# Recurrence of a two-block transformer: the last solution's bank products ahead of the second scores, the key norm's steps spread over two weight blocks each, a pair's last outputs behind the next pair's first scores

## The chip, the cores and the metric

The kernel runs on one NeuronCore of one Trainium2 chip. The core has a matrix engine (TensorE, PE in the profile), a vector engine (VectorE, DVE), an activation engine (ScalarE, ACT), a general engine (GpSimd, POOL) and a queue of transfers that SyncE (SP) issues. The metric is the device time of one execution in microseconds.

## The reference

The kernel computes two transformer blocks over 512 tokens of width 1024, all in 32-bit floats. The first block has a recurrence with a delta rule (RWKV7), 12 heads of 64, beside an attention to 256 memory tokens, and then a feed-forward of width 4096. The second has two local attentions with gates and a gated feed-forward. The change touches the recurrence alone, and one number that the plan keeps from there to the end. Cut to what matters:

```python
proj = h @ w_in                                   # 512x1024 by 1024x2560 (and the memory's queries)
slab = proj + (shifted(proj) - proj) * mu         # token shift: each token takes part of the one before
r, k, v, wd, ad, gd = split(slab)                 # r, k, v: 768 each, 12 heads of 64
decay = exp(-exp(-softplus(-(w0 + tanh(wd) @ w2)) - 0.5))
a  = sigmoid(a0 + ad @ a2);  g = sigmoid(gd) @ g2
kk = normalised(k * k_k);    k = k * (1 + (a - 1) * k_a)
for t in range(512):                              # per head, S is 64x64
    S = S * decay[t] + outer(S @ -kk[t], kk[t] * a[t]) + outer(v[t], k[t])
    y[t] = S @ r[t]
y = group_norm(y) * g1 + b1
mix = (y + sum(r * k * r_k) * v) * g
x = x + concat(mix, memory_attention) @ w_out
```

## The kernel before

**Weights.** The weights come in 216 units, most of them 128 rows by 1024 columns. SP loads a unit into `Wraw`, ScalarE casts it to the reduced format fp32r (`Whi`, line 2090), and VectorE or POOL subtracts to get the rest (`Wlo`, line 1643 on VectorE, 2418 on POOL). Cast and subtraction together are one *split*. Its loads run in a ring of `NW` = 3 sets. During the recurrence the plan gives all subtractions to POOL (`state["lo"] = "wlo_pool"`). A unit makes one output tile of 128x512 by eight *weight blocks*; a block is three matmuls of 128x512 (`Hhi,Whi`, `Hlo,Whi`, `Hhi,Wlo`). A tile of kind `slab` is one third (r, k or v, in the plan `projection(p, 0)`, `(p, 1)`, `(p, 2)`) of what a pair of heads needs. When it is done, VectorE scales it (evict, line 1700: `ftmp<-bank,RS`), ScalarE multiplies by a vector (line 2155: `slab<-ftmp,VD`) and VectorE adds the shifted neighbour (`shift`, line 1774: `slab<-ftmp,V,slab`).

**Recurrence.** The 512 tokens are eight chunks of 64 and the 12 heads six pairs (`NP` = 6, `NC` = 8). Inside a chunk the recurrence is solved with products of 64x64, which all lie on line 1047 of PE; one `bank` is a 128x512 piece of PSUM. For a pair the plan has four generators. `inverse(p)` makes the scores (`xm`, `sb`, `na`, `nb`, `vn`, `kn`, `sk`), a triangular inverse in six levels (`t1`, `xt`, `xu` with the level's number), `gv`, and at its end `yu`, a level product. `states(p)` makes the last solution `uw` (`GA,Yi`), the increments `pd`, the transfers `phi`, the outputs in chunks `yo1`, seven state steps `st`, in each of which PE waits for the state `PD` of the step before (line 1915), and the outputs from the states, `yo2`. `tail(p)` makes the group norm (`gsq`, `root t`, `tn`), the gate `tg` (`GD,g2s`) and the result `tlo`. `bonus(p)` is the step `bo`. `ahead(p + 1)` prepares the next pair: the three projections, and between them `sg` and `ta` (decay and rate), the square of the key (`sq`), the running sum of the decays (`cum`, the scan of line 1791), `exps`, `kf`, the root of the key norm (`root f`), `kk` and `ops` (four VectorE instructions of the operands, lines 1805 to 1820, and the product kf*Pi on POOL, line 2476). VectorE masks what PE has written: line 1829 (`BR<-bank,C`) reads the second scores `sb`, line 1879 makes `T`, line 1886 makes `Xi`, both for a level of the inverse.

**Order.** The plan is one list of steps, made at build time; each engine runs its part of the list in order, and waits on semaphores where a step needs another engine's result. `two("sb", p)` takes two of the five PSUM banks of ring `M`, in turn, so a step waits also for the bank's former user to be read out. `inverse(p)` sets the pace: each `yield` of it gives a number of microseconds, and `blend` lets the filler emit as many steps as fit in that number times `FILL_PAIR`. The filler alternates (`turns`) between two lines of steps: bonus, states and tail of the pair behind, and `ahead(p + 1)`. In the loop over pairs, what is left of the filler is emitted at the end of the pair:

```python
gens = [itertools.chain(bonus(p), *((states(p - 1), tail(p - 1)) if p else ())), ahead(p + 1)]
filler = turns(*gens)
blend(inverse(p), filler, FILL_PAIR[p])
run(filler)
```

A split is put in the list when a unit begins: `splits(u + state["ahead"])`. With `ahead` = 2 (`NW - 1`) the split of the next unit is queued then, with 3 (`NW`) that of the one behind it. The five stretches of the loop are called pairs here: the first lies at 64 to 107 us, the others at about 107, 156, 204 and 253 us to 303 us.

Of the kernel before, what the change touches and what calls it, by code (L numbers as in the profile page):

```python
# [14 lines left out]
NP = 6  # L15
# [3 lines left out]
FILL_PAIR = (1.05, 1.35, 1.35, 1.35, 1.35)  # L19
# [6 lines left out]
NW = 3  # L26
# [34 lines left out]
class Plan:  # L61
# [9 lines left out]
    def step(self, kind, *key):  # L71
        self.steps.append((kind, *key))
        self.count(kind, *key)
# [55 lines left out]
def run(gen):  # L129
    for _ in gen:  # L130
        pass


def turns(*gens):
    gens = list(gens)
    while gens:
        for g in list(gens):
            try:
                yield next(g)
            except StopIteration:  # L140
                gens.remove(g)
# [31 lines left out]
def blend(main, filler, per):  # L173

    due = 0.0
    for room in main:
        due += per * room
        while due > 0:
            took = next(filler, None)
            if took is None:  # L180
                break
            due -= took


def couples(tile):

    for _ in tile:
        next(tile, None)
        yield 1.6
# [7 lines left out]
def make_plan(units):  # L197
# [9 lines left out]
    state = {"loads": 0, "splits": 0, "units": 0, "lo": "wlo", "ahead": 1, "held": None}  # L207
# [29 lines left out]
    def bank(kind, *key):  # L237

        M.take((kind, *key))
        step(kind, *key)  # L240
        M.give((kind, *key))
# [94 lines left out]
    def shift(t):  # L336

        step("shift", t)
        ftmp.give(("shift", t))
# [118 lines left out]
        yield from pipeline([item(n) for n in range(8)])  # L458

    def projection(p, i):  # L460
        state["held"] = held = []
        yield from couples(tile("slab", (p, i), ("rw", 6 * i + p), "x", range(8)))
        state["held"] = None
        yield 0
        shift(held[0])

    def rates(p):

# [14 lines left out]
    def bonus(p):  # L483
        step("bo", p)
        ftmp.give(("sq", p))
        yield 1.0

    def ahead(p):

        k = projection(p, 1)  # L490
        for _ in range(4):
            yield next(k)
        yield from rates(p)
        yield from k
        square(p)
        r = projection(p, 0)
        yield next(r)
        decays(p)
        yield next(r)
        step("exps", p)  # L500
        step("kf", p)
        bank("root", "f", p)
        yield 0.9
        yield from r
        v = projection(p, 2)
        yield next(v)
        bank("kk", p)
        yield 0.5
        yield next(v)
        step("ops", p)  # L510
        yield next(v)
        yield from v

    def inverse(p):

        two("xm", p)
        yield 1.4
        two("sb", p)
        yield 0.9
        two("na", p)  # L520
        yield 0.7
        for kind in ("nb", "vn", "kn"):
            bank(kind, p)
            yield 0.7
        two("sk", p)
        step("ai", p)
        yield 1.0
        for l in range(1, len(LEVELS)):
            if l == 3:
                two("gv", p)  # L530
                yield 0.7
            two("t1", p, l)
            if l > 1:
                two("xt", p, l - 1)
            yield 1.6
            if l < len(LEVELS) - 1:
                two("xu", p, l)
                yield 1.4
        bank("yu", p)
        yield 1.2  # L540

    def states(p, room=0.2):

        two("uw", p)
        yield 1.0
        two("pd", p)
        yield 0.5
        two("phi", p)
        yield 0.6
        two("yo1", p)  # L550
        yield 0.6
        for ch in range(1, NC - 1):
            step("st", p, ch)
            yield room
        bank("yo2", p)
        yield 0.9

    def tail(p):
        step("gsq", p)
        yield 0  # L560
        bank("root", "t", p)
        yield 0.9
        yield 0
        bank("tn", p)
        yield 0.5
        yield 0
        bank("tg", p)
        yield 1.0
        step("tlo", p)
        count("Ulo", "mix", p)  # L570
        yield 0


    def values_and_queries():
        yield from projection(0, 2)
        for i in range(2):
            yield from couples(tile("qm", (i,), ("rw", 20 + i), "x", range(8)))

# [26 lines left out]
    filler = between()  # L605
# [7 lines left out]
    state["lo"] = "wlo_pool"  # L613
    mem_att = mem_attention()
    mix_order = (0, 1, 2, 3, 4, 6, 7, 5)
    for p in range(NP - 1):
        gens = [itertools.chain(bonus(p), *((states(p - 1), tail(p - 1)) if p else ())), ahead(p + 1)]
        filler = turns(*gens)
        blend(inverse(p), filler, FILL_PAIR[p])
        run(filler)  # L620

    outs = [tile("res", ("gffn", i), ("wo", i), "mix", mix_order, js=mix_order, own=i == 2) for i in range(3)]

    def beside():
        yield from turns(itertools.chain(bonus(NP - 1), states(NP - 2), tail(NP - 2)), mem_att)
        step("Xload")
        for i, g in enumerate(outs):

            state["ahead"] = (NW - 1, NW, NW - 1)[i]
            yield from spaced(itertools.islice(g, 7), 0.8)  # L630
        state["ahead"] = NW - 1

    filler = beside()
    blend(itertools.chain(inverse(NP - 1), states(NP - 1, 0.6), spaced(tail(NP - 1), 1)), filler, FILL_LAST)
# [82 lines left out]
    filler = some_gates(range(8))  # L717
# [14 lines left out]
    filler = side_b()  # L732
# [2017 lines left out]
```

## Time and profile before

| | us |
|---|---|
| median of three runs | 1522.12 |
| lowest, highest | 1521.64, 1524.64 |
| the profiled execution | 1518.95 |
| its span in the trace | 1517.2 |

| engine | busy us | share of the span | instructions |
|---|---|---|---|
| PE, matmuls | 1462.2 | 96% | 11374 |
| PEld, weight loads (beside PE) | 1156.8 | 76% | 11374 |
| DVE | 800.4 | 53% | 1261 |
| ACT | 552.7 | 36% | 942 |
| POOL | 239.4 | 16% | 166 |

The span is the time from the first to the last record of the core; the profiled execution's own time is 1.75 us above it. The share of an engine is the mean over all stages. A wait of PE is idle time that the profile puts down to what came last, as in `[1.79 <-DVE BR L1829]`. The granted clock (PEclk) is 1.00 at 2.4 GHz and 0.50 at 1.2 GHz; over the whole span it is 0.997.

### The profile page before, as it was taken

Reading aid. Unit: us, or ns where it says so; the run is one execution under the profiler, and the core shown is the slowest. Engines: PE = TensorE matmul, PEld = TensorE weight load, DVE = VectorE, ACT = ScalarE, POOL = GpSimd, SP = SyncE. Lnnn points to the kernel's source line nnn. Section 1 sums busy time; section 2 is a strip of 40 time slices with the busy share of each in tenths; the row PEclk is TensorE's granted clock in tenths of the full one; section 3 lists DMA queues with packets and bytes.
Section 4 is the critical chain, followed back from the end, with each engine's and each line's share of the span. In section 5 each row is a group of like instructions: output and inputs, shape, how many; then the busy total and the mean of one; then the engine's idle time right before and its main releaser. Section 6 shows DMA issues by size and latency. Waiting matters only on the chain.

```text
span 1517.2 us, 26650 instructions
## 1 busy us (share of the span) xinstructions
PE 1462.2 (96%) x11374; PEld 1156.8 (76%) x11374; DVE 800.4 (53%) x1261; ACT 552.7 (36%) x942; POOL 239.4 (16%) x166
## 2 busy tenths in 40 slices
PE   7999999979999999999999999999999999999999
PEld 6867777756788888888788766767777888888887
DVE  5655566664564444535644358577554443443343
ACT  7444434363422221312442256545333221222221
POOL 0233333201200000000110012222322210220120
PEclk9999999999999999999999999999999999999999
DMA  8311011011223232333233133311222333323223
GB/s 323 112 30 44 30 30 44 23 52 58 70 87 108 84 108 87 98 97 97 84 97 96 58 107 96 94 56 53 83 92 89 97 97 98 97 85 109 84 88 107
DMA packets 39334, 130.89 MB, mean 86 GB/s; under 512 B 4272, under 2 KB 5296, under 8 KB 39216
## 3 DMA queue, kind: packets, MB, share of 16 engines
q1 hardware_dynamic: 39216, 129.18, 26.9%
q8 instruction: 90, 1.47, 0.4%
q14 instruction: 28, 0.23, 0.0%
HBM read 127.07 MB, written 2.10 MB: 85 GB/s over the span
## 4 chain that ended last, share of the span: by engine, by line
PE 82%; DVE 8%; ACT 4%; issue 3%; POOL 0%; POOLq 0%; ACTq 0%; DVEq 0%
PE bank L1047 79%; PE bank L1447 1%; DVE Wlo L1643 1%; ACT Whi L2090 1%; DVE qa L1754 1%; DVE z L1680 0%; DVE Xi L1886 0%; DVE qa L1752 0%; ACT Hhi L2171 0%; PE bank L1161 0%; DVE X L1725 0%; ACT kbr L2337 0%; ACT slab L2306 0%; PE bank L1237 0%; ACT tmpb L2205 0%
## 5 line engine op out<-in xcount | busy, mean ns | idle before, releaser
L1047 PE MATMUL bank<-Hhi,Whi 128*128 128x512 f32 x912 | 375.8, 412 | 11.6 <-DVE Wlo L1643 8.4
L1047 PE MATMUL bank<-Hhi,Wlo 128*128 128x512 f32 x912 | 360.9, 396 | 0.0
L1047 PE MATMUL bank<-Hlo,Whi 128*128 128x512 f32 x912 | 357.6, 392 | 0.0
L1047 PE MATMUL bank<-Uhi,Whi 128*128 128x512 f32 x736 | 290.9, 395 | 8.1 <-POOL Wlo L2418 3.1
L1047 PE MATMUL bank<-Uhi,Wlo 128*128 128x512 f32 x736 | 287.2, 390 | 0.0
L1047 PE MATMUL bank<-Ulo,Whi 128*128 128x512 f32 x736 | 287.0, 390 | 0.0
L2090 ACT CAST Whi<-Wraw 128x1024 fp32r<-128x1024 f32 (+1 forms) x216 | 222.9, 1036 | 164.2 <-PE bank L1047 148.2
L1643 DVE TENSOR_TENSOR Wlo<-Wraw,Whi 128x1024 fp32r<-128x1024 f32 (+1 forms) x175 | 224.2, 1282 | 98.9 <-ACT Whi L2090 98.8
L1047 PEld LDWEIGHTS bank<-Hhi,Whi 128*128 128x128 f32 x912 | 171.5, 188 | 66.0 <-issue 12.3
L1047 PEld LDWEIGHTS bank<-Hlo,Whi 128*128 128x128 f32 x912 | 171.9, 188 | 42.1
L1047 PEld LDWEIGHTS bank<-Hhi,Wlo 128*128 128x128 f32 x912 | 172.0, 189 | 34.0 <-issue 1.2
L1047 PEld LDWEIGHTS bank<-Uhi,Whi 128*128 128x128 f32 x736 | 138.1, 188 | 45.2 <-DVE Wlo L1643 5.5
L1047 PEld LDWEIGHTS bank<-Ulo,Whi 128*128 128x128 f32 x736 | 138.3, 188 | 29.4
L1047 PEld LDWEIGHTS bank<-Uhi,Wlo 128*128 128x128 f32 x736 | 138.3, 188 | 27.8 <-issue 0.2
L2418 POOL TENSOR_TENSOR Wlo<-Wraw,Whi 128x1024 fp32r<-128x1024 f32 x41 | 99.8, 2433 | 367.1 <-ACT Whi L2090 366.4
L1725 DVE TENSOR_TENSOR X<-X,bank 128x512 f32<-128x512 f32 x72 | 49.5, 688 | 168.8 <-PE bank L1047 168.7
L2426 POOL TENSOR_TENSOR accb<-accb,tmpb 128x512 f32<-128x512 f32 x14 | 18.8, 1344 | 383.9 <-ACT tmpb L2205 383.9
L2165 ACT CAST Uhi<-tmpb 128x512 fp32r<-128x512 f32 x32 | 19.8, 619 | 148.0 <-DVE tmpb L1734 148.0
L2431 POOL TENSOR_TENSOR qa<-qa 128x512 f32<-128x512 f32 x22 | 28.5, 1295 | 198.9 <-ACT qa L2175 198.9
L2179 ACT CAST Hhi<-qa 128x512 fp32r<-128x512 f32 x22 | 13.7, 622 | 116.0 <-POOL qa L2436 116.0
L2347 ACT ACTIVATE sr<-sr,st 128x256 f32<-128x256 f32 (+1 forms) x64 | 33.7, 528 | 36.6 <-DVE st L2015 19.8
L1732 DVE SCALAR_TENSOR_TENSOR tmpb<-bank,RSb 128x512 f32<-128x512 f32 x32 | 22.1, 692 | 44.8 <-PE bank L1047 44.6
(292 smaller groups left out, 1571.8 us busy)
## 6 DMA issues: line engine op xcount, KB each, us to landing
Wraw<-in_wts SPq DMA_DIRECT2D x208, 512.0 KB, 3.5
bA<-in_biasA SPq DMA_DIRECT2D x12, 256.0 KB, 2.8
Wraw<-in_wts SPq DMA_DIRECT2D x8, 384.0 KB, 3.2
x<-in_xT SPq DMA_DIRECT2D x8, 256.0 KB, 4.4
x_rows<-in_xN SPq DMA_DIRECT2D x2, 1024.0 KB, 8.3
X<-in_xT SPq DMA_DIRECT2D x2, 1024.0 KB, 7.2
out<-X SPq DMA_DIRECT2D x8, 256.0 KB, 2.1
bB<-in_biasB SPq DMA_DIRECT2D x4, 384.0 KB, 3.1
```

The source lines that it names most:

```text
L1047: return e.matmul(o, lhsT, rhs, start=start, stop=stop, skip_group_check=True)
L1447: p = e.transpose(o, sr[n % 3][:, x:x + 128], c("ident"))
L1643: e.tensor_tensor(Wsp[k][1][:, 0:width], Wraw[k][:, 0:width], Wsp[k][0][:, 0:width].bitcast(F), ALU.subtract).then_inc(S["wlo"])
L1725: e.tensor_tensor(y, y, z, ALU.add).then_inc(S["evict"])
L1732: e.scalar_tensor_tensor(z[:], b[:], 0.0, RSb[:], ALU.max, ALU.mult).then_inc(S["evict"])
L1754: e.tensor_tensor(z[:], z[:], gates[i], ALU.add).then_inc(S["gated"])
L2090: e.copy(Wsp[k][0][:, 0:width], Wraw[k][:, 0:width]).then_inc(S["whi"])
L2165: e.copy(Uhi[:, x.key[1], :], tmp_of(("raw", t))[:]).then_inc(S["ffhi"])
L2347: p = e.activation(part, part, ACT.Exp, scale=1.0, bias=x[:, 2 + i:3 + i], accum_out=x[:, 4 + i:5 + i])
L2418: done(e.tensor_tensor(Wsp[k][1][:, 0:width], Wraw[k][:, 0:width], Wsp[k][0][:, 0:width].bitcast(F), ALU.subtract), "wlo_pool")
L2426: done(e.tensor_tensor(accb[:], accb[:], tmp_of(("sqr", *x.key))[:], ALU.add), "sq_add")
L2431: done(e.tensor_tensor(z[:], z[:], s[:], ALU.mult), "sig")
```

## The change

It has five parts.

1. `inverse(p)`: for all pairs but the last, the room behind `xm` goes from 1.4 to 2.0 and that behind `sb` from 0.9 to 0.3. The filler's step `uw` of the pair behind then stands between the two weight blocks and `sb`, in place of behind `sb`.
2. `ahead(p)`: k, r and v are generators whose steps are couples of two weight blocks, and every other step of the next pair stands behind one couple. `read_out` finishes a tile and emits its evict; the shift comes behind the next tile's first couple.
3. The loop over pairs emits at a pair's end only what is left of the projections. What is left of the chain (bonus, states, tail) goes on beside the next pair's first steps. The last state steps, `yo2`, `gsq` and `root t` then have other neighbours among the weight blocks.
4. `values_and_queries`, ahead of the first pair, gets the same form.
5. `state["ahead"]` is `NW` from the end of the recurrence on, in place of `NW - 1`.

```diff
--- before.py
+++ after.py
@@ -458,11 +458,14 @@
         yield from pipeline([item(n) for n in range(8)])
 
     def projection(p, i):
+        return couples(tile("slab", (p, i), ("rw", 6 * i + p), "x", range(8)))
+
+    def read_out(projected):
+
         state["held"] = held = []
-        yield from couples(tile("slab", (p, i), ("rw", 6 * i + p), "x", range(8)))
+        run(projected)
         state["held"] = None
-        yield 0
-        shift(held[0])
+        return held[0]
 
     def rates(p):
 
@@ -487,36 +490,40 @@
 
     def ahead(p):
 
-        k = projection(p, 1)
+        k, r, v = (projection(p, i) for i in (1, 0, 2))
         for _ in range(4):
             yield next(k)
         yield from rates(p)
-        yield from k
+        t = read_out(k)
+        yield next(r)
+        shift(t)
         square(p)
-        r = projection(p, 0)
-        yield next(r)
         decays(p)
         yield next(r)
         step("exps", p)
         step("kf", p)
+        yield next(r)
         bank("root", "f", p)
-        yield 0.9
-        yield from r
-        v = projection(p, 2)
+        yield next(r)
+        t = read_out(r)
+        yield next(v)
+        shift(t)
         yield next(v)
         bank("kk", p)
-        yield 0.5
         yield next(v)
         step("ops", p)
         yield next(v)
-        yield from v
+        t = read_out(v)
+        yield 0
+        shift(t)
 
     def inverse(p):
 
         two("xm", p)
-        yield 1.4
+
+        yield 2.0 if p < NP - 1 else 1.4
         two("sb", p)
-        yield 0.9
+        yield 0.3 if p < NP - 1 else 0.9
         two("na", p)
         yield 0.7
         for kind in ("nb", "vn", "kn"):
@@ -572,7 +579,11 @@
 
 
     def values_and_queries():
-        yield from projection(0, 2)
+        v = projection(0, 2)
+        yield from itertools.islice(v, 4)
+        t = read_out(v)
+        yield 0
+        shift(t)
         for i in range(2):
             yield from couples(tile("qm", (i,), ("rw", 20 + i), "x", range(8)))
 
@@ -613,22 +624,25 @@
     state["lo"] = "wlo_pool"
     mem_att = mem_attention()
     mix_order = (0, 1, 2, 3, 4, 6, 7, 5)
+    rest = iter(())
     for p in range(NP - 1):
-        gens = [itertools.chain(bonus(p), *((states(p - 1), tail(p - 1)) if p else ())), ahead(p + 1)]
-        filler = turns(*gens)
-        blend(inverse(p), filler, FILL_PAIR[p])
-        run(filler)
+
+        chain = itertools.chain(rest, bonus(p), *((states(p - 1), tail(p - 1)) if p else ()))
+        projections = ahead(p + 1)
+        blend(inverse(p), turns(chain, projections), FILL_PAIR[p])
+        run(projections)
+        rest = chain
 
     outs = [tile("res", ("gffn", i), ("wo", i), "mix", mix_order, js=mix_order, own=i == 2) for i in range(3)]
 
     def beside():
-        yield from turns(itertools.chain(bonus(NP - 1), states(NP - 2), tail(NP - 2)), mem_att)
+        yield from turns(itertools.chain(rest, bonus(NP - 1), states(NP - 2), tail(NP - 2)), mem_att)
         step("Xload")
         for i, g in enumerate(outs):
 
             state["ahead"] = (NW - 1, NW, NW - 1)[i]
             yield from spaced(itertools.islice(g, 7), 0.8)
-        state["ahead"] = NW - 1
+        state["ahead"] = NW
 
     filler = beside()
     blend(itertools.chain(inverse(NP - 1), states(NP - 1, 0.6), spaced(tail(NP - 1), 1)), filler, FILL_LAST)
```

On PE, at the start of a steady pair: `ftmp,C` is the bonus `bo`, the `Hhi`/`Hlo` rows are the first of two weight blocks (the second reads the same), `AR,ta` is `sb`, `GA,Yi` is `uw`, `C,AR` is `na`. Before:

```order
L1047 MATMUL bank<-GD,g2s 128x512
L1047 MATMUL bank<-ta,AR_125 64x64 x16
L1047 MATMUL bank<-ftmp_76,C 128x512
L1047 MATMUL bank<-Hhi,Whi_61 128x512
L1047 MATMUL bank<-Hhi,Wlo_62 128x512
L1047 MATMUL bank<-Hlo,Whi_61 128x512
...
L1047 MATMUL bank<-AR_125,ta 64x128 x16
L1047 MATMUL bank<-GA_108,Yi_109 64x128 x16
L1047 MATMUL bank<-C,AR_125 64x64 x16
```

After:

```order
L1061 MATMUL bank<-ta,AR_125 64x64 x16
L1061 MATMUL bank<-ftmp_76,C 128x512
L1061 MATMUL bank<-Hhi,Whi_61 128x512
L1061 MATMUL bank<-Hhi,Wlo_62 128x512
L1061 MATMUL bank<-Hlo,Whi_61 128x512
...
L1061 MATMUL bank<-GA_108,Yi_109 64x128 x16
L1061 MATMUL bank<-AR_125,ta 64x128 x16
L1061 MATMUL bank<-C,AR_125 64x64 x16
```

`uw` now stands ahead of `sb`; the gate product `GD,g2s` stood ahead of `xm` (`ta,AR`) before, and stands ahead of `yu` (`Yi,T`) now.

On PE, at the end of the pair before that: the last rows are a weight block, `yu` (`Yi,T`), `tg` (`GD,g2s`), `xm` and `bo`. Before:

```order
L1047 MATMUL bank<-Hhi,Whi_59 128x512
L1047 MATMUL bank<-Hhi,Wlo_60 128x512
L1047 MATMUL bank<-Hlo,Whi_59 128x512
L1047 MATMUL bank<-Yi_109,T_119 64x64 x16
L1047 MATMUL bank<-GD,g2s 128x512
L1047 MATMUL bank<-ta,AR_125 64x64 x16
L1047 MATMUL bank<-ftmp_76,C 128x512
```

After (`Xi,MT` is the last `t1`, `C,Xi` the last `xt`, the first `C,z` is the sum of `root t` and the second, on another line, the mean `tn`):

```order
L1061 MATMUL bank<-Xi,MT 64x64 x16
L1061 MATMUL bank<-C,Xi 64x64 x16
L1061 MATMUL bank<-C,z_106 128x128 x4
L1175 MATMUL bank<-C,z_106 128x128 x4
L1061 MATMUL bank<-GD,g2s 128x512
L1061 MATMUL bank<-Yi_109,T_119 64x64 x16
L1061 MATMUL bank<-ta,AR_125 64x64 x16
```

The weight block that stood right ahead of `yu` is gone from there; between the last `t1` and `xm` PE has bank products only.

On DVE, around the scan of the next pair's decays (`sg<-C,sg`), with the state steps `PD`, the evict `ftmp<-bank,RS` and the shift. Before:

```order
L1915 SCALAR_TENSOR_TENSOR PD<-bank,PC_89,PD 128x64
L1700 TENSOR_TENSOR ftmp_77<-bank,RS 128x512
L1915 SCALAR_TENSOR_TENSOR PD<-bank,PC_89,PD 128x64
L1774 SCALAR_TENSOR_TENSOR slab_69<-ftmp_77,V,slab_69 128x511
L1879 TENSOR_TENSOR T_119<-bank,C 128x4x64 x2
L1915 SCALAR_TENSOR_TENSOR PD<-bank,PC_89,PD 128x64
L1791 SCALAR_TENSOR_TENSOR sg<-C,sg 128x512
L1886 TENSOR_TENSOR Xi<-bank,Xi 128x4x64 x2
```

After:

```order
L1929 SCALAR_TENSOR_TENSOR PD<-bank,PC_89,PD 128x64
L1714 TENSOR_TENSOR ftmp_77<-bank,RS 128x512
L1893 TENSOR_TENSOR T_119<-bank,C 128x4x64 x2
L1929 SCALAR_TENSOR_TENSOR PD<-bank,PC_89,PD 128x64
L1788 SCALAR_TENSOR_TENSOR slab_69<-ftmp_77,V,slab_69 128x511
L1805 SCALAR_TENSOR_TENSOR sg<-C,sg 128x512
L1900 TENSOR_TENSOR Xi<-bank,Xi 128x4x64 x2
L1929 SCALAR_TENSOR_TENSOR PD<-bank,PC_89,PD 128x64 x2
```

Before, the mask `T` and a state step stood between the shift and the scan; now the shift and the scan stand next to each other, behind the mask and one state step more.

On ScalarE, at the same place, the square of the key (`ftmp<-slab`) stood between the multiply `slab<-ftmp` and the cast `Whi` of the next unit. Now the cast comes right behind the multiply, and the square behind it and a copy of `Yi`.

## Rows read from the trace of the kernel before

**Rows 1.** Stretches of three pairs: length, busy us per engine, PEclk, DMA, GB/s.

```profile
64.00:107.09 43.09, 41.07 (x756) 32.17 (x758) 24.47 (x51) 17.95 (x35) 13.20 (x11) 1.00 0.17 52
...
204.20:252.81 48.61, 45.08 (x965) 34.98 (x964) 30.40 (x65) 20.26 (x40) 16.11 (x12) 1.00 0.11 35
252.81:302.97 50.16, 46.63 (x966) 36.27 (x965) 30.40 (x65) 20.26 (x40) 16.10 (x12) 0.97 0.09 25
```

**Rows 2.** Waits of PE, 107 to 303 us: total us, times, longest.

```profile
PE bank L1047 <- DVE BR L1829: 7.2, 4, 1.8
PE bank L1047 <- DVE PD L1915: 3.8, 4, 1.0
PE bank L1047 <- DVE Xi L1886: 2.7, 4, 0.7
```

**Rows 3.** Timeline from 204 us: start, length, engine, operation, [idle before].

```profile
207.27 1.10 PE L1047 MATMUL bank<-AR,ta 64*64 64x128 f32 x32
...
210.46 0.76 DVE L1829 TENSOR_TENSOR BR<-bank,C 128x256 f32<-128x256 f32 x2
...
211.03 0.69 PE L1047 MATMUL bank<-C,AR 64*64 64x64 f32 x32 [1.79 <-DVE BR L1829]
```

**Rows 4.** Timeline, 224 to 227 us, the first state steps of a pair.

```profile
224.34 0.29 PE L1047 MATMUL bank<-PD,AR 64*64 64x64 f32 x4
...
225.26 0.27 DVE L1915 SCALAR_TENSOR_TENSOR PD<-bank,PC,PD 128x64 f32<-128x64 f32 x1
...
225.59 0.33 PE L1047 MATMUL bank<-PD,AR 64*64 64x64 f32 x4 [0.96 <-DVE PD L1915]
...
226.16 0.72 ACT L2155 ACTIVATE slab<-ftmp,VD 128x512 f32<-128x512 f32 x1
```

**Rows 5.** Timeline, 242 to 252.6 us, the end of that pair.

```profile
242.56 2.38 POOL L2418 TENSOR_TENSOR Wlo<-Wraw,Whi 128x1024 fp32r<-128x1024 f32 x1 [8.32 <-ACT Whi L2090]
...
243.15 0.69 PE L1047 MATMUL bank<-T,Yi 64*64 64x64 f32 x32
...
243.55 1.67 DVE L1680 COPY z<-st 128x512 f32<-128x512 f32 x1
...
245.28 0.66 PE L1161 MATMUL bank<-C,z 128*128 128x128 f32 x4
...
246.60 0.69 PE L1047 MATMUL bank<-Xi,MT 64*64 64x64 f32 x32 [0.67 <-DVE Xi L1886]
...
247.69 0.50 PE L1047 MATMUL bank<-Hhi,Whi 128*128 128x512 f32 x1
...
247.91 0.75 DVE L1879 TENSOR_TENSOR T<-bank,C 128x256 f32<-128x256 f32 x2
...
248.57 0.68 DVE L1820 TENSOR_TENSOR AR<-kn,Pp 128x512 f32<-128x512 f32 x1
...
250.38 0.74 DVE L1805 SCALAR_TENSOR_TENSOR ftmp<-slab,V,kf 128x512 f32<-128x512 f32 x1
...
251.25 1.27 POOL L2476 TENSOR_TENSOR kf<-kf,Pi 128x512 f32<-128x512 f32 x1 [4.02 <-DVE ftmp L1805]
```

**Rows 6.** Timeline, 101 to 104 us and 229 to 233 us.

```profile
101.64 1.29 POOL L2470 TENSOR_TENSOR ta<-ta,kn 128x512 f32<-128x512 f32 x1
...
101.92 1.55 DVE L1820 TENSOR_TENSOR AR<-kn,Pp 128x512 f32<-128x512 f32 x1
...
229.06 1.21 DVE L1791 TENSOR_TENSOR_SCAN sg<-C,sg 128x512 f32<-128x512 f32 x1
...
229.51 2.92 POOL L2418 TENSOR_TENSOR Wlo<-Wraw,Whi 128x1024 fp32r<-128x1024 f32 x1 [2.39 <-ACT Whi L2090]
```

**Rows 7.** Waits of PE, 372 to 1517 us.

```profile
PE bank L1047 <- POOL Wlo L2418: 6.2, 4, 1.7
PE bank L1047 <- DVE Wlo L1643: 2.8, 3, 1.8
```

**Rows 8.** The stretch with the low granted clock, columns as in rows 1.

```profile
262.00:264.00 2.00, 2.00 (x9) 1.70 (x9) 0.00 (x0) 0.26 (x1) 0.00 (x0) 0.50 0.49 195
```

## The prediction, made before the changed kernel ran

> **What bounds the kernel now.** I read the totals of five stretches first. TensorE (PE) is busy in about 93% of a pair [rows 1], so the end can only move by the stretches in which PE stands. The first pair of heads lies at 64 to 107 us; of the next four, three take 48.6 us and the last 50.16. The list of waits for those four pairs has three entries that repeat in all four [rows 2]: 7.2 us for the BR mask, 3.8 us for the state PD, 2.7 us for Xi. I call them gaps A, B and C. In order of time they are 1.79 us before the `na` products [rows 3], 0.96 us before the second state product [rows 4], 0.67 us before the last `t1` [rows 5]. Together 1.79 + 0.96 + 0.67 = 3.42 us a pair. Behind 372 us, PE's waits for a split weight are 6.2 + 2.8 us [rows 7].
>
> **Part 1, solution ahead of second scores.** `uw` now takes the two banks behind `tn` and `tg`, `sb` takes one behind `yu` and one behind `xm`, and `na` waits for the second `xm` bank and the first `uw` bank. All these are read out early, so `na` no longer waits for VectorE's (DVE's) seven `sb` masks. What is late next: `vn` takes the first `sb` bank and needs six of the seven masks. Before, the masks end at 210.46 + 0.76 = 211.22, about 2.8 us behind the end of `sb` (207.27 + 1.10) [rows 3]; the sixth ends some 0.35 us sooner. Between `sb` and `vn` PE now has `na` (0.69), two weight blocks (about 1.5) and `nb` (about 0.4), so at most 0.1 us of gap A stays. `uw` also needs the sum Yi behind `yu`; DVE does it some 5.0 us behind the start of `tn`, and PE comes to `uw` at 5.8. Gain 1.7 us a pair; bounds 0.9 (Yi a DVE step late) to 1.79.
>
> **Part 2, one chain step later.** The second state product moves from right behind the first to behind two weight blocks, `t1` and `xt`, about 2.6 us, against the 1.2 us that it needs from first product to PD [rows 4]. Gap B goes: 0.96 us, bounds 0.8 to 0.96.
>
> **Part 3, the end of a pair.** Before, four weight blocks stand between the last `xt` and `yu`; now two of them stand ahead of the last `t1`, and the other two further forward. So behind the last block PE has `t1`, `xt`, `root t`, `tn`, `tg`, `yu`, `xm` and nothing to fill. Call S the start of the last `xu`. PE: from S to behind two blocks 245.28 - 243.15 = 2.13 us, `t1` and `xt` 247.69 - 246.60 = 1.09, `root t` about 1.2: idle from S + 4.4 [rows 5]. DVE: Xi from about S + 0.75 to S + 1.45, then the four of `ops`, from 248.57 to 250.38 + 0.74 = 2.55 us, which now stand ahead of the last mask: S + 4.0; mask 0.75: S + 4.75; then reciprocal and the copy into z, which without a disturbance takes 0.4 us (one measured 1.67 only since a split of POOL stood beside it) [rows 5]. POOL's kf*Pi starts 0.13 behind `ops` and takes 1.27 [rows 5], so it is over at S + 5.4, and the copy ends at about S + 5.75. `tn` starts at S + 5.8: a new wait of 1.4 us where gap C was 0.67. I take 1.5, bounds 0.9 (the mask hides some) and 2.7 (copy as before, 1.67). Gap C goes, since between `xu` and `t1` no key multiply stands ahead of Xi any more. In the first pair the end costs about the same as the 1.04 and 0.70 us that PE waits there now (not shown apart: 43.09 - 41.07 = 2.0 us idle [rows 1]).
>
> **Part 4, POOL's split beside the scan.** This is the step that decides. Shift and square of the key come later, but the cast of the next weight stays right behind the key's first slab. In ScalarE's queue the square no longer stands ahead of the cast. The slab starts at 226.16 [rows 4], the cast follows about 0.65 later and POOL's subtraction (Wlo) 1.1 after that: 227.9, not 229.51 as now [rows 6]. DVE then has, back to back, PD, the shift (slab<-ftmp,V,slab) from about 227.8 and the scan. Both read two tensors of SBUF. What such an overlap does: AR<-kn,Pp took 1.55 us beside a POOL multiply that had started 0.28 earlier [rows 6], and 0.68 alone [rows 5]; it ended 0.54 behind POOL. The other way round, Wlo beside the scan took 2.92 us, where another took 2.38 [rows 6, 5]. So whoever is first holds the other up. If the shift is first, by 0.1 us, Wlo stands waiting while it runs, and I expect it to be next: Wlo from about 228.5 to 230.9 and the scan over at about 232.0, where alone it would end at 229.7. Xi and the next PD stand behind it on DVE: PD at 233.0, and the fourth state product, whose slot on PE is at 231.9, waits 1.2 us. If Wlo is first the shift waits and the wait is 1.0. If DVE keeps its hold over both, none. I take 1.2 us, bounds 0 and 2.4 (a whole Wlo). In the first pair there is no state product, but the exponents and with them the key norm's copy and a mask come 2.3 us later: about 0.9 us more.
>
> The Trainium skill, "SBUF — State Buffer", section "Who interferes with whom", says that a DVE instruction with two SBUF inputs contends with a GpSimd one that reads SBUF, and elsewhere on that page that the first to start holds the shared ports for the whole instruction. The 1.55 us of [rows 6] agree. By that rule the change loses its 1.2 us; without it, none.
>
> **Part 5, casts one weight earlier.** From here on each split is queued a whole weight ahead of its use. What PE can gain is its two shorter waits for DVE's Wlo, 2.8 - 1.8 = 1.0 us [rows 7], some four of 0.1 at 740 to 780, and of the waits for POOL's Wlo near 1100 (the longest is 1.7 us) little: there POOL holds up DVE's gate sums, and PE would next wait for DVE's evictions, so I take 0.4. The 1.8 us wait at 392 stays: two splits in place of one stand behind the same three evictions. Sum 1.8 us; bounds 0 and 6.
>
> **Sum.** The profiled execution took 1518.95 us (span 1517.2). Four pairs: 4 x (3.42 - 0.1 - 1.5 - 1.2) = 2.5 us; first pair -0.9; part 5 +1.8. Saved 3.4, so 1515.5 for an execution like that one. The median of the timed runs is 3.17 us above it: 1518.7. The clock fell once in the pairs, to 0.50 (1.2 GHz) at 262 to 264 us [rows 8], behind a gap A, and that pair took 50.16 instead of 48.61 [rows 1]. With gap A gone I give that 1.55 us half a chance to go: 0.8. **Forecast 1518.0 us.** The term with the widest bounds is the fourth. With parts 1 to 3 at the better ends, part 4 at 0 and part 5 at 1.8, 4 x 2.5 + 1.8 + 0.8 = 12.6 us are saved: 1509.5. With part 4 at 2.4 and part 3 at 2.7, 4 x (3.42 - 0.1 - 2.7 - 2.4) - 0.9 + 1.8 = -6.2: 1528.3.
>
> **Rivals.** (a) *DVE keeps its hold, the scan isn't delayed.* For it: the shift starts, by my times, just ahead of Wlo, and the scan follows it with no wait. Against: when DVE's hold ends, POOL has been waiting. Then 4 x (3.42 - 0.1 - 1.5) + 1.8 + 0.8 = 9.9: 1512.2 us.
> (b) *The end of a pair is worse than 1.5 us.* z's copy stands beside a POOL instruction as long as now, 1.67 instead of 0.4, in four pairs: 5 us against (a) or the forecast. Against: no split is due there, since the cast behind the last slab comes later. With part 4 at its forecast the four pairs gain nothing, -0.9 + 1.8 + 0.8 = 1.7 less 2.5: 1522.9; with part 4 at 0 it is 1517.3.
> (c) *Slower: the clock.* From the last `t1` to `bo` PE now has some 7 us with a wait in it and no weight block. A gap of 1.8 us was followed by half clock in one pair of four [rows 1, 8], priced 1.55 us. Should the clock fall twice in each of the five pairs, 10 x 1.55 = 15.5 less the forecast's 3.4: 1534. It decides from three falls on: 3.4 us saved and 2 x 1.55 more than now. Against: the wait is shorter than gap A, and B is gone.
> (d) *It doesn't do what it says.* The order shows the moved products; banks alone could still hold `uw` back if `tn`'s read-out on DVE is late (part 1's margin is 0.8 us). Then A is only moved: 4 x 0.9 less than forecast, 1521.6.
>
> **How the numbers follow.** Forecast as summed: 0.47; (a) 0.28; (b) 0.09; (c) 0.08; (d) 0.08. 0.2% of 1522 is 3.0 us, about what a measurement of this kernel tells from no change. The forecast stands 4.1 us below, and its own range of 1515 to 1521 lies two thirds under that bound; with (a) that gives faster 0.63, same 0.26 (a third of the forecast, most of (b) and (d)), slower 0.11. The range takes in (a) and most of (b) and (d) and leaves out (c): 1511 to 1523.
>
> **What would show it.** Right: no PE wait behind the BR mask, nor for PD behind the first state product; a PE wait of 1.3 to 1.6 us for the copy into z at each of four pair ends; the scan or the shift at 2 us or more instead of 1.2 or 0.75, with Wlo across it, and a PE wait for PD of about 1.2 us; pairs of about 47.8 us. Pairs of 46.6 us with a 2.9 us or longer Wlo mean (a). Pairs of 48.6 us or more, with a granted clock under 1, mean (c). Wrong in any case: a wait at `uw`, or pair spans over 49 us at full clock.

## The result: 1508.37 us, faster by 0.96%, outside the forecast range

| | median us | lowest, highest | runs |
|---|---|---|---|
| before | 1523.03 | 1521.64, 1524.64 | 4 |
| after | 1508.37 | 1507.47, 1509.41 | 4 |

The ratio is 0.9904, with a 95% interval of 0.9886 to 0.9921. A second set of runs of the same kernel gave 1509.69 against 1522.02, 0.9919 (0.9905 to 0.9934). The gain is 12 to 15 us; the forecast had 4, and a lowest value of 1511. The profiled execution of after took 1509.15 us (span 1507.3), 9.8 us less than that of before.

The totals of the stretches in after (columns as in [rows 1]): the first pair with 5 us of what lies ahead of it, a steady pair, and the last pair up to the second output tile.

```profile
64.00:107.82 43.82, 41.53 (x755) 32.61 (x754) 26.14 (x52) 19.26 (x37) 13.57 (x11) 1.00 0.20 60
201.45:248.26 46.81, 44.66 (x971) 34.66 (x969) 30.97 (x66) 20.50 (x40) 16.54 (x12) 1.00 0.12 37
...
295.04:386.18 91.14, 77.12 (x1360) 56.75 (x1356) 50.42 (x122) 40.91 (x95) 12.94 (x8) 0.96 0.10 32
```

A pair takes 46.8 us where [rows 1] has 48.61. PE waits 1.3 us less in it, and its own busy time is 0.42 us less (45.08 to 44.66). PE's waits from 107 to 295 us in after answer to [rows 2]:

```profile
PE bank L1175 <- DVE z L1694: 5.4, 4, 1.4
PE bank L1061 <- DVE PD L1929: 3.1, 4, 0.8
PE bank L1061 <- DVE T L1893: 1.4, 1, 1.4
```

The waits behind BR, for the first PD and for Xi are gone. In their place stand two: 1.35 us for z's copy at each pair's end, and 0.78 us for a later PD. (The single wait for T is the end of the first pair.) The timeline of after at the start of a pair answers to [rows 3]:

```profile
204.57 1.10 PE L1061 MATMUL bank<-GA,Yi 64*64 64x128 f32 x32
...
205.50 1.05 PE L1061 MATMUL bank<-AR,ta 64*64 64x128 f32 x32
...
206.47 0.69 PE L1061 MATMUL bank<-C,AR 64*64 64x64 f32 x32
...
208.64 0.76 DVE L1843 TENSOR_TENSOR BR<-bank,C 128x256 f32<-128x256 f32 x2
...
210.27 0.35 PE L1061 MATMUL bank<-GA,BR 64*64 64x64 f32 x8
```

`uw`, `sb` and `na` follow each other with no wait, and the last two masks of `sb` (208.64) are done before anything needs them. The next place is around the scan, in the same view; it answers to [rows 4, 6]:

```profile
223.46 0.74 DVE L1788 SCALAR_TENSOR_TENSOR slab<-ftmp,V,slab 128x511 f32<-128x511 f32 x1
223.59 2.85 POOL L2432 TENSOR_TENSOR Wlo<-Wraw,Whi 128x1024 fp32r<-128x1024 f32 x1 [0.78 <-ACT Whi L2104]
...
224.12 3.42 DVE L1805 TENSOR_TENSOR_SCAN sg<-C,sg 128x512 f32<-128x512 f32 x1
...
228.10 0.27 DVE L1929 SCALAR_TENSOR_TENSOR PD<-bank,PC,PD 128x64 f32<-128x64 f32 x1
...
228.42 0.33 PE L1061 MATMUL bank<-PD,AR 64*64 64x64 f32 x4 [0.78 <-DVE PD L1929]
```

The shift starts 0.13 us ahead of POOL's subtraction and takes 0.74 us (0.75 where nothing stands beside it, in e11 below). The scan behind it takes 3.42 us in place of 1.21: it ends 1.1 us behind the subtraction, as if it had begun only when that was over. And at the end of a pair, answering to [rows 5]:

```profile
244.06 0.75 DVE L1893 TENSOR_TENSOR T<-bank,C 128x256 f32<-128x256 f32 x2
244.28 1.26 POOL L2490 TENSOR_TENSOR kf<-kf,Pi 128x512 f32<-128x512 f32 x1 [3.29 <-DVE ftmp L1819]
...
245.02 0.20 DVE L1691 RECIPROCAL st<-st 128x8 f32<-128x8 f32 x1 [0.20 <-ACT st L2147]
245.25 0.57 DVE L1694 COPY z<-st 128x512 f32<-128x512 f32 x1
...
245.97 0.63 PE L1175 MATMUL bank<-C,z 128*128 128x128 f32 x4 [1.35 <-DVE z L1694]
```

PE's waits behind 366 us in after. Those for POOL's `Wlo` of [rows 7] (6.2 us) are not in the list; others, for VectorE's gate sums, stand at the same places, so that these lists alone show no gain (13 us in both kernels). The wait for `sr`, 2.2 us here, is 0.4 us in before (last row).

```profile
PE bank L1061 <- DVE qa L1766: 2.9, 2, 1.6
...
PE bank L1061 <- DVE sr L2016: 2.2, 1, 2.2
PE bank L1061 <- DVE Wlo L1657: 1.8, 1, 1.8
PE bank L1061 <- DVE Hlo L1770: 1.8, 1, 1.8
```

```profile
PE bank L1047 <- DVE sr L2002: 0.4, 1, 0.4
```

### The profile page after: what moved, and what is told of

Same layout as the page of the kernel before. It is cut to its first block, busy times and chain, and to the rows that moved or that the text cites. A ratio compares the mean times of both kernels' runs of the same rounds, so it can differ in the third digit from the quotient of the medians.

```text
span 1507.3 us, 26652 instructions
## 1 busy us (share of the span) xinstructions
PE 1458.5 (97%) x11374; PEld 1157.6 (77%) x11374; DVE 809.5 (54%) x1261; ACT 554.1 (37%) x942; POOL 241.5 (16%) x166
## 3 DMA queue, kind: packets, MB, share of 16 engines
q8 instruction: 90, 1.47, 0.4%
## 4 chain that ended last, share of the span: by engine, by line
PE 85%; DVE 7%; ACT 2%; issue 2%; POOL 0%; POOLq 0%; ACTq 0%; DVEq 0%
PE bank L1061 82%; PE bank L1461 1%; DVE sg L1805 1%; DVE qa L1768 1%; PE bank L1175 1%; DVE qa L1766 0%; ACT Hhi L2185 0%; DVE Wlo L1657 0%; PE bank L1418 0%; ACT kbr L2351 0%; ACT slab L2320 0%; PE bank L1251 0%; DVE T L1893 0%; ACT Whi L2104 0%; DVE Xi L1900 0%
```

## The experiments

All ratios are to before, from runs on the same chip, made together. A *fall* is a stretch in which the granted clock is 0.50 (1.2 GHz). The theory after the result was: the order of `uw` carries nearly all of the pairs' gain, falls of the clock that follow gap A carry the rest, and parts 2 to 4 cancel. Its rivals: that before's profiled execution was merely a quick one, and that the new order of the whole pair is what helps.

### c0: the kernel before, again

No edit.

> The unchanged kernel, to see how its executions differ. The profiled execution of before took 1518.95 us and its timed runs 1521.6 to 1524.6, while after has 1507.5 to 1509.4 with its profiled one among them. Theory (clock): each wait of 1.8 us behind the second scores is followed by a fall to half clock in some executions; the profiled one had 1 in four pairs, the others have 2 to 4 in the pairs, at 1.55 us each. Then a run of 1523 shows a mean granted clock about 0.001 lower per 1.6 us, 0.994 to 0.996 where the first showed 0.997. Rival (other): the clock is 0.997 in slow and quick runs alike and the 4 us lie in waits.

Measured: 1521.13 us (1518.65 to 1523.75, 12 runs) against 1521.55, 0.9998 (0.9988 to 1.0009). Of the 32 executions of before in this set, those with a mean granted clock of 0.995 or less (14 of them) took 1522.9 us on average, those with 0.997 or more (14 too) 1519.3, and four lie between. So the kernel before has two groups of executions, and the profiled one of the forecast (0.997, 1518.95) was of the quick one. The profiled execution here has its fall at another place, behind the third gap A, and its pair takes 50.13 us where its neighbours take 48.55:

```profile
204.59:254.72 50.13, 46.60 (x965) 36.28 (x964) 30.41 (x65) 20.26 (x40) 16.08 (x12) 0.97 0.11 34
212.00:214.00 2.00, 2.00 (x13) 1.57 (x6) 0.00 (x0) 0.65 (x2) 1.32 (x2) 0.61 0.40 94
214.00:216.00 2.00, 2.00 (x10) 1.74 (x9) 0.00 (x0) 0.43 (x1) 0.00 (x0) 0.54 0.45 176
```

The theory's price holds (1.55 to 1.6 us a fall); that the longer executions have their falls in the pairs is not shown, since only profiled executions show where a fall lies.

### e1 and e2: part 5 alone

```diff
 # e1, from after
-        state["ahead"] = NW
+        state["ahead"] = NW - 1
```

```diff
 # e2, from before
-        state["ahead"] = NW - 1
+        state["ahead"] = NW
```

> After, with only the casts' distance behind the recurrence put back (2 in place of 3). In the traces the two kernels lie 5.87 us apart from 392 to 740 us and 9.8 us at the end. Theory (casts): those 3.9 us are part 5's, so this kernel is 3 to 4.5 us slower than after, 1511.3 to 1512.9, and the waits for Wlo of POOL near 1100 (6.2 us in all) are back. Forecast's own figure: 1.8 us, 1510.2. Rival (chance of one execution): under 1 us apart, since the clock fell elsewhere there.

> Before, with only the casts' distance behind the recurrence changed (3 in place of 2). Theory: as large as in e1 with the sign turned, 3 to 4.5 us under before, 1518.5 to 1520. Rival (forecast): 1.8 us. Rival (chance): under 1 us.

Measured: e1 1512.43 us (1510.68 to 1514.03), 0.9937 (0.9922 to 0.9952), which by the ratios is 2.7 us above the second set of after and 5.0 above the first; e2 1518.23 us (1516.28 to 1519.86), 0.9977 (0.9966 to 0.9988), 3.3 us under before. Part 5 is worth 3.3 us or a little more, not 1.8: of the executions with a mean granted clock of 0.995, three of e1 take 1513.7 us on average and three of after 1509.6. Where it lies is seen in the same work in both traces (the first two rows are of before, the last two of after; the first of each starts at the same weight block, and so does the second):

```profile
724.32:982.40 258.08, 254.16 (x1281) 194.43 (x1280) 144.70 (x226) 118.38 (x219) 33.32 (x17) 1.00 0.30 91
1160.51:1517.20 356.69, 352.83 (x1537) 287.87 (x1535) 142.57 (x154) 88.74 (x108) 56.53 (x44) 1.00 0.30 95
```

```profile
718.45:974.71 256.26, 252.33 (x1281) 195.38 (x1280) 143.96 (x225) 118.12 (x219) 33.24 (x17) 1.00 0.30 91
1152.50:1507.30 354.80, 351.59 (x1537) 288.31 (x1535) 143.23 (x153) 87.95 (x107) 56.33 (x44) 1.00 0.30 94
```

1.82 and 1.89 us less, and this is no chance of two executions. From the first matmul of each stretch to the first behind it, or to the last of all, the four traces without part 5 take 258.1 us (c0, with a fall, 259.6) and 352.8 to 353.1; the ten traces with it take 256.2 to 256.3 and 351.3. In both stretches it is mostly PE's *busy* time that shrinks (1.83 and 1.24 us), though the matmuls are the same. A split that comes a little late doesn't stand in the list of waits; it stretches the distance of two matmuls. Before:

```profile
739.33 1.63 DVE L1643 TENSOR_TENSOR Wlo<-Wraw,Whi 128x1024 fp32r<-128x1024 f32 x1 [0.60 <-ACT Whi L2090]
...
740.50 0.39 PE L1047 MATMUL bank<-Ulo,Whi 128*128 128x512 f32 x1
...
741.02 0.50 PE L1047 MATMUL bank<-Uhi,Whi 128*128 128x512 f32 x1
...
741.36 0.39 PE L1047 MATMUL bank<-Uhi,Wlo 128*128 128x512 f32 x1
```

The subtraction ends at 740.96, and the two matmuls behind it start 0.52 and 0.34 us after the matmul ahead of each, in place of 0.23. No wait of PE is listed there. At the same two places e1 has 0.52 and 0.34 too, e2 and after 0.23 and 0.23. The beginnings of the seven weights between 735 and 770 us make 1.5 of the first stretch's 1.82 us in this way. In the second stretch two such places, one of them with a listed wait of 0.52 us, make 1.1 us; the rest is spread over some 1500 distances of 0.23 us, and its cause is open. The end of the 1.47 us wait for POOL's `Wlo` at 897 us brought nothing: the wait for `sr` behind it grew from 0.42 to 2.18 us.

### e3, e6 and e8: the place of uw

```diff
 # e3, from before; e8 is e3 with the edit of e2
-        yield 1.4
+        yield 2.0 if p < NP - 1 else 1.4
         two("sb", p)
-        yield 0.9
+        yield 0.3 if p < NP - 1 else 0.9
```

e6 is after with these two lines as they are in before.

> Before, with only the last solution uw put ahead of the second scores sb in four pairs. Theory: the 1.79 us wait behind BR goes in each of four pairs and nothing takes its place, 7.2 us; with the falls of the clock that follow it (1 to 3 of 1.55 us) 8 to 11 us under before: 1512 to 1515. Pairs of 46.8 us in the trace, no half clock between 107 and 300 us. Rival (moved wait): uw waits for Yi or for its banks, half or more stays, 3.6 us or less gained, 1519. Rival (no clock): 7.0 to 7.4 us, 1516.

> After, with uw behind sb again in its four pairs and nothing else undone. e3 and e8 say that the order of uw carries the result. Theory: the wait for the seventh mask of sb is back, 1.7 to 1.8 us in each of four pairs, pairs of 48.5 us, and with it the falls to half clock in the pairs: 1.67 * 4 = 6.7 plus 1.5 to 3, so 8 to 10 us above after, 1517 to 1519, 0.9975 of before. Rival (the new order of the other steps has its own cover for it): under 1.0 us a pair, 1512.

> Before, with uw ahead of sb in four pairs and the casts' distance 3 behind the recurrence, and nothing else of the change. By the single runs uw brings 9.6 us and the casts 3.3 to 4. Theory (parts 2 and 3 bring nothing: -0.14 us in each of four pairs, -0.07 in the first, +1.2 in the last by the traces): as quick as after within 1 us, 1508 to 1509.5. Rival (parts 2 and 3 bring what the forecast had for them, or more than it): 2 us or more behind after.

Measured: e3 1511.97 us (1509.54 to 1513.61), 0.9936 (0.9922 to 0.995), 9.6 us under before. e6 1518.48 us (1516.66 to 1523.65), 0.9983 (0.9972 to 0.9995). e8 1509.28 us (1507.10 to 1511.71), 0.9919 (0.9905 to 0.9934), beside after's 1509.69 with the same 0.9919. Waits of PE in the pairs, first of e3, then of e6:

```profile
PE bank L1047 <- DVE PD L1915: 3.8, 4, 1.0
PE bank L1047 <- DVE Xi L1886: 2.7, 4, 0.7
...
```

```profile
PE bank L1061 <- DVE BR L1843: 7.8, 4, 2.0
PE bank L1175 <- DVE z L1694: 5.4, 4, 1.3
PE bank L1061 <- DVE PD L1929: 3.1, 4, 0.8
```

In e3 gap A is gone and nothing is in its place; B and C stand as before. In e6 it is back, at 1.8 to 2.0 us, beside the two new waits. The steady pair of e3:

```profile
202.29:249.22 46.93, 45.16 (x965) 35.01 (x965) 30.41 (x65) 20.27 (x40) 16.13 (x12) 1.00 0.12 36
```

46.93 us against 46.81 in after: all that parts 2 to 4 do in a steady pair is 0.12 us. And e8 has what the whole change has. My expectation for e8 laid 1.2 us in the last pair on parts 2 and 3. That stands for parts 2 to 4: with two falls in it the last pair takes 89.91 us in e3 and 91.14, 91.08 and 91.12 in after, a1 and e1. The profiled execution of e8 takes 91.2 us there too, but with three falls. But for e5 and e10 the last pair took 89.1 to 91.2 us in all the traces, with one to three falls of the clock in it.

The traces bear on the clock as well. The four profiled executions of kernels with gap A (before, c0, e2, e6) have one fall to 0.50 each in the four steady pairs, within 4 us behind a gap A; in the ten executions of kernels without it there is none there (after, a1, e1, e3 to e5, e8 to e11). Falls come at other places in every kernel, at least one of them in the last pair. e3's six runs have mean clocks of 0.997 to 0.999, 0.998 on average. But the ten runs of after, which has no gap A either, have 0.996 on average, and the 67 of before 0.995: how much of the clock gap A costs over a whole execution is open.

### a1, e4, e9 and e11: POOL's subtraction beside DVE

a1 is after again, the measure for e4.

```diff
 # e4, from after; e9 does the same around shift(t) of r
         t = read_out(k)
+        state["ahead"] -= 1
         yield next(r)
+        state["ahead"] += 1
         shift(t)
         square(p)
         decays(p)
+        splits(state["units"] - 1 + state["ahead"])
```

```diff
 # e11, from e4
         t = read_out(r)
-        yield next(v)
         shift(t)
+        yield next(v)
         yield next(v)
```

> The changed kernel again, as the measure for the three beside it on one chip: 1507.5 to 1509.5, pairs of 46.8 us, 0.9910 of before.

> After, with the load, cast and POOL subtraction of the unit behind the r unit queued behind the shift, the square and the scan, in place of ahead of them; in all five pairs. In after the scan takes 3.42 us beside a 2.85 us subtraction, and PE waits 0.78 us for the state PD behind it. Theory (contention, part 4): the scan is back at about 1.2 us and the subtraction at 2.4, the 0.78 us wait for PD is gone, pairs of 46.0 us, and 3.1 us less in all, 1504.5 to 1506. Rival (the scan's length has another cause, such as its place behind the shift): it stays over 2 us, pairs of 46.8 us. Rival (slack): the scan is short, but the wait only moves to the next state step or to kk, 46.5 us.

> e4, and also the load and split of the unit behind the v unit queued behind the shift of r. In e4 the scan was back at 1.22 us and its POOL subtraction at 2.39, but the shift of r, which in after had started 0.07 us ahead of its subtraction and taken 0.74, now started 0.34 us behind it and took 2.58, and PE waited 0.30 us. Theory (whoever of DVE and POOL is first holds the other up to its end): shift of r 0.75, both subtractions 2.4, the 0.30 us wait gone, pairs of 45.8 to 45.9 us, 1.2 us under e4, 1505.5 to 1506.5. Rival: the casts now come too late on ScalarE for the weights, or copies of Yi and T wait behind them, pairs of 46.2 us or more.

> e4, and the shift of r directly behind its evict, in place of behind the last state step but one. In e9 the plan's later split moved nothing: ScalarE had no other work that waits there, its cast began at 231.01 as in e4, the subtraction at 232.12, the shift at 232.46, and the shift took 2.58 us. Now DVE comes to the shift at 231.1, as soon as ScalarE's multiply is done, a whole 1.0 us ahead of the subtraction. Theory (who is first): shift 0.75, Xi (which reads PSUM) 0.26 us later than in e4 but 0.8 ahead of its use, kk's wait of 0.30 us gone, pairs of 45.8 to 45.9 us, 1.2 us under e4, 0.9895 to 0.990 of before. Rival (the subtraction now meets Xi or PD and makes one of them long instead): a wait of 0.3 us or more in the same place, pairs of 46.15 us or more.

Measured: a1 1509.69 us, 0.9919 (0.9905 to 0.9934); e4 1507.15 us (1504.82 to 1509.42), 0.9905 (0.9889 to 0.9921); e9 1505.80 us, 0.9897 (0.9885 to 0.9910); e11 1504.61 us (1503.41 to 1506.76), 0.9892 (0.9873 to 0.9911). Of e4 the two places where POOL's subtraction and a DVE instruction come near each other:

```profile
221.91 1.22 DVE L1808 TENSOR_TENSOR_SCAN sg<-C,sg 128x512 f32<-128x512 f32 x1
...
223.83 2.39 POOL L2435 TENSOR_TENSOR Wlo<-Wraw,Whi 128x1024 fp32r<-128x1024 f32 x1 [3.23 <-ACT Whi L2107]
...
232.04 2.38 POOL L2435 TENSOR_TENSOR Wlo<-Wraw,Whi 128x1024 fp32r<-128x1024 f32 x1 [4.01 <-ACT Whi L2107]
...
232.38 2.58 DVE L1791 SCALAR_TENSOR_TENSOR slab<-ftmp,V,slab 128x511 f32<-128x511 f32 x1
```

With the subtraction 1.92 us behind the scan's start both are back at their own length, the wait for PD is gone, and the pair takes 46.2 us. But the shift of r now starts 0.34 us *behind* its subtraction and takes 2.58 us. e9 was meant to mend that and did nothing of the kind: ScalarE has no other work there that waits, so its cast began as early as in e4 although the plan named it later, the shift still took 2.58 us, and its pairs of 46.15 us are e4's; its runs have a higher mean clock than e4's (0.997 against 0.996). The same two places in e11:

```profile
220.98 1.22 DVE L1808 TENSOR_TENSOR_SCAN sg<-C,sg 128x512 f32<-128x512 f32 x1
...
222.90 2.38 POOL L2435 TENSOR_TENSOR Wlo<-Wraw,Whi 128x1024 fp32r<-128x1024 f32 x1 [3.22 <-ACT Whi L2107]
...
230.11 0.75 DVE L1791 SCALAR_TENSOR_TENSOR slab<-ftmp,V,slab 128x511 f32<-128x511 f32 x1 [0.79 <-ACT slab L2172]
...
231.09 2.39 POOL L2435 TENSOR_TENSOR Wlo<-Wraw,Whi 128x1024 fp32r<-128x1024 f32 x1 [4.00 <-ACT Whi L2107]
```

Here the shift is over before the subtraction begins. PE's only wait in the steady pairs of e11 is that for z; a pair takes 45.76 us:

```profile
PE bank L1178 <- DVE z L1697: 5.4, 4, 1.4
```

```profile
196.47:242.23 45.76, 44.40 (x966) 34.55 (x965) 29.02 (x66) 20.62 (x40) 15.61 (x12) 1.00 0.12 37
```

So the overlap costs after 46.81 - 45.76 = 1.05 us a pair and 0.5 us in the first (38.34 against 37.84 us between its `xm` and the next). e11 is quicker than both kernels of the case; against after the ratios differ by 0.1 to 0.3% (0.9892 beside 0.9904 and 0.9919), which the intervals alone don't settle. The traces do so for the pairs: each of the four steady ones takes 45.8 us in e11 and 46.8 in after and a1.

### e5 and e10: the end of a pair

```diff
 # e5, from after; e10 is e9 with this and with tlo behind the next xm
             two("t1", p, l)
             if l > 1:
                 two("xt", p, l - 1)
-            yield 1.6
+            yield 1.6 if l < len(LEVELS) - 1 or p == NP - 1 else 0.7
...
         bank("yu", p)
-        yield 1.2
+        yield 1.2 if p == NP - 1 else 2.1
```

> After, with the level product yu ahead of the group norm's tn in place of behind it and tg, which is all that moves in the steady pairs. Theory (part 3: PE has nothing ready at a pair's end): yu's 0.87 us of work falls into tn's wait of 1.35 us, which shrinks to 0.4 to 0.6; pairs of 45.9 to 46.1 us; 3 to 3.6 us less in all, 1504.5 to 1506. Rival (the DVE line is what binds): yu's sum Yi now stands ahead of z's copy or of the evict on DVE and holds up tn and uw by as much, pairs of 46.8 us or more.

> e9, with yu ahead of tn as in e5, and the last step of a pair's outputs (tlo, its cast and the VectorE subtraction Ulo) behind xm of the next pair. In e5 yu did fill the 1.35 us wait, but sb then waited 1.41 us for the mask of xm, which stood behind Ulo on DVE, and Ulo had waited 0.68 for ScalarE's cast. Theory: with Ulo (0.69) and its wait (0.68) behind the mask, sb's wait is gone or under 0.2 us: 1.0 us a pair under e9, pairs of 44.8 to 45.0 us, 1501.5 to 1503. Rival (DVE has no slack there at all: the evict, the shift, three steps of y and Yi stand ahead of the mask anyway): sb waits 0.7 us or more and the pair is no better than e9's 45.8.

Measured: e5 1513.76 us (1511.57 to 1517.19), 0.9948 (0.9934 to 0.9962), 4 us *above* after; e10 1506.18 us (1505.43 to 1508.57), 0.9903 (0.9890 to 0.9916). Of e5 the end of one pair and the start of the next:

```profile
246.22 1.15 PE L1061 MATMUL bank<-Yi,T 64*64 64x64 f32 x32 [0.34 <-DVE T L1893]
...
247.30 0.66 PE L1175 MATMUL bank<-C,z 128*128 128x128 f32 x4
...
253.16 0.69 DVE L1953 TENSOR_TENSOR Ulo<-y,Uhi 128x512 fp32r<-128x512 f32 x1 [0.68 <-ACT Uhi L2306]
...
253.77 0.75 DVE L1843 TENSOR_TENSOR Xi<-bank,C 128x256 f32<-128x256 f32 x2
...
254.33 0.89 PE L1061 MATMUL bank<-AR,ta 64*64 64x128 f32 x24 [1.41 <-DVE Xi L1843]
```

`yu` did fill the wait for z, of which 0.34 us is left. But DVE then has the evict, the shift, three steps of y and Ulo between `tn` and the mask of `xm`, and PE waits 1.41 us for that mask. The first steady pair, with no `tlo` at its start, takes 46.0 us, the other three 47.6, which is 1.6 us more than after in all. The rest of the 4 us fits the clock, though no run isolates it: e5's profiled execution has as much time at 0.50 in the last pair as four falls, a1's as two. e10 puts Ulo behind the mask; the wait becomes 0.3 to 0.6 us, for ScalarE's copy GA, and its pairs take 46.07 us, no better than e9's 46.15. This bears the rival out: from `root t` to `sb` it is DVE's and ScalarE's line that sets the time, and PE's idle 1.35 us is slack of that line.

## Why the prediction was wrong, step by step

The mechanisms of parts 1 to 4 were the right ones. What failed is the counting of a stretch by its listed waits alone (in the pairs and in part 5), the price of part 4, the last pair, which stood at nothing, and the constant between trace and median. The sum was mis-sized by 5.6 us in the traces (4.2 forecast with the clock's 0.8, 9.8 found) and by 4.0 us more in going from them to the median, 9.6 in all. The largest piece of the 5.6 is the four pairs: 1.81 us found against 0.62 forecast in each, 4.8 us in all. Of the 1.19 us, 0.5 is the missing term below, 0.4 the price of part 4, and the rest part 3's wait and the 0.1 of gap A that went too.

- **Part 1** (gap A). Held: e3 takes gap A away from before, e6 puts it back into after. Forecast 1.7 us a pair, found 48.61 - 46.93 = 1.68 in e3. No wait at `vn`, none at `uw`; rival (d) is out.
- **Part 2** (gap B). Held: that wait is gone, and the one for a later PD that stands in after is part 4's, since it goes with the overlap in e4.
- **Part 3** (end of a pair). Forecast a wait of 1.5 us, found 1.35. z's copy took 0.57 us, not 1.67; rival (b) is out.
- **Part 4** (POOL beside the scan). The mechanism held to a tenth of a microsecond: shift first, the scan 2.2 us late (2.3 forecast). Its price did not: PE waits 0.78 us, where 1.2 was forecast. PE came to the state product 0.1 us behind the scan's end (228.42 - 0.78 = 227.64), where I had it 0.1 ahead, and PD was there 0.83 us behind that end, where I had 1.0. What the overlap costs in all, by e11, is 1.05 us a pair, one more shift included. In the first pair it costs 0.5 (0.9 forecast), and that pair gained 0.07 us in all, where a loss of 0.9 was forecast. Rival (a) is out, by the scan's 3.42 us; the sign that I gave for it, pairs of 46.6 us with a 2.9 us `Wlo`, nearly came true (46.8 and 2.85) and would have misled.
- **The term that was missing.** The waits of a pair fell by 3.42 - 2.13 = 1.29 us and the pair by 1.81: 0.5 us is in PE's busy time (0.42) and in a gap too short for the list. I had counted a pair as its listed waits and nothing else. e3, whose other products stand in the old order, has 45.16 us busy, after 44.66: so it belongs to parts 2 to 4, and it is what makes them break even with their two new waits. Which neighbours among the products cost it isn't settled.
- **Part 5.** The step that failed was "What PE can gain is its two shorter waits": listed waits again. Those two waits did go (2.8 to 1.8 us), and the waits for POOL's `Wlo` gave way to others, as forecast. But e2 has 3.3 us, and 1.5 of them stand at seven places where before has no listed wait at all, for which I had taken some four of 0.1.
- **The last pair.** It stood at nothing in the sum, without a reason. It takes 91.14 us in after and 89.11 in before, with a fall more (1.55 us), and beside e3, at equal falls, 1.2 us are lost in it. What loses them isn't settled.
- **The clock in the pairs.** Forecast half a chance of 1.55 us from one execution. By the traces the fall is there in four of four profiled executions with gap A and in none of ten without it. Rival (c), that the new gaps would bring falls of their own in the pairs, is out. In the last pair after had two falls where before had one, and over the whole span both profiled executions have three, so the traces' 9.8 us hold next to nothing of the clock.
- **From trace to median.** I added 3.17 us to an execution like the profiled one. For before the median lay 4.1 us above it (1523.03 - 1518.95), for after 0.8 below its own (1508.37 - 1509.15). The offset isn't a constant of the kernel: it was the distance from a quick execution to the usual one. e3 shows it: 4 x 1.68 = 6.7 us of waits, and 9.6 us between the medians. At an equal mean clock of 0.998 three runs of e3 take 1511.7 us and three of before 1518.6, 6.9 us apart: what is above the waits is the clock's mix. That the mix changed with gap A is not shown, since after's runs, without gap A, have a lower clock than e3's.

Sum of what was found at an equal number of falls: 4 x 1.81 + 0.07 + 1.82 + 1.89 (part 5) = 11.0 us, and 0.3 more between the two stretches of part 5; the last pair takes back 0.5 to 1.2. The medians lie 12.3 and 14.7 us apart. The record settles most of that: at a mean clock of 0.998 three runs of before take 1518.6 us and four of after 1507.2, 11.4 apart, and at 0.995 it is 12.3 (two and three runs; the runs of before are from several sets). The rest is in the clock's mix.

The "rest of a pair's outputs behind the next first scores" did nothing: the plan's list of steps is the same with the rest run out at the pair's end, since nothing is left of it there.

## What to carry to other kernels

A list of waits bounds what a new order can bring from neither side. A listed wait can give way to another one at the same place, as 6.2 us for POOL's `Wlo` did, and a weight that is a little late stands in the busy time. Compare the busy time and the length of the same stretch of work as well. When one profiled execution lies at the edge of the timed runs, ask which clock group it is of before adding a constant to it. And where a VectorE instruction with two SBUF inputs may meet a POOL one, settle in the order who is first: in e11 a shift that started 1 us ahead of the subtraction, not 0.34 behind it, took 0.75 us in place of 2.58.

## What the runs showed that I had not expected

Three overlaps show the same rule in numbers, and it is a sharp one. Shift 0.13 us ahead of the subtraction (after): shift 0.74 us, as alone, subtraction 2.85 against 2.39. Scan right behind that shift, while the subtraction was waiting or running: 3.42 against 1.22, so VectorE did not keep its hold from one instruction to the next. Shift 0.34 us behind the subtraction (e4): 2.58 against 0.75, over 0.5 us behind the subtraction's end, which stays at 2.38. The VectorE instructions that read PSUM and one SBUF tensor (Xi 0.75 us, PD 0.27 and 0.28) kept their length beside the subtraction in e11. The Trainium skill, "SBUF — State Buffer", section "Who interferes with whom", says that a VectorE instruction with two SBUF inputs contends with a GpSimd one that reads SBUF, that one with at most one SBUF input (outside the modes that use two ports) does not, and that the order of issue decides who is blocked. The traces agree in all of these cases.

The busy time of PE isn't its work: the same 1537 matmuls took 352.83 us busy in before and 351.59 in after, at a granted clock of 1.00 in both. Part of that is late weights that stand in no list of waits, as at 741 us.
